# Raw k, q and v of a delta rule turned by transfers and block transposes, in place of TensorE transposes, with the scan two tiles later

## What is computed

```
qkv = silu(causal_depthwise_conv(concat([q, k, v]), conv_w))      # 4 taps along the tokens
q, k = l2_normalize(q) * DN_DK**-0.5, l2_normalize(k)
# in chunks of 64 tokens, g = cumsum(log decay), decay = exp(g_c - g_s) on c >= s
a_mat = strict_lower((k*beta) @ k.T * decay)
u, w = triangular_solve(a_mat + I, [v*beta, k*beta*exp(g)])
qk = (q @ k.T) * decay
# step over the chunks
v_new = u - w @ S ;  o = (q*exp(g)) @ S + qk @ v_new ;  S = S*g_tot + k_tail.T @ v_new
o = rms_norm(o) * silu(z)
```

## Time and profile before

| | us |
|---|---|
| median of 3 runs | 1929.85 (1929.77 to 1930.6) |
| the profiled execution | 1930.64 |
| its span, first to last instruction | 1928.8 |
| TensorE busy | 1913.5 (99%) |
| VectorE busy | 1330.6 (69%) |
| ScalarE busy | 928.9 (48%) |
| GpSimd busy | 101.3 (5%) |

### The profile page before, as it was taken

The page is one execution under the profiler, slowest core; times in us unless marked ns, Lnnn a source line. Parts: engine busy times, 40 slices in busy tenths (PEclk is TensorE's granted clock), DMA queues, the critical chain, the costliest instruction groups (busy, mean ns, idle before and its releaser), DMA issues.

```text
span 1928.8 us, 31440 instructions
## 1 busy us (share of the span) xinstructions
PE 1913.5 (99%) x10359; PEld 1574.6 (82%) x10359; DVE 1330.6 (69%) x1872; ACT 928.9 (48%) x1308; POOL 101.3 (5%) x296
## 2 busy tenths in 40 slices
PE   9999999999999999999999999999999999999997
PEld 7788888888888888888888887888888888888886
DVE  7868688786757777776566756577675466665656
ACT  5555564554455555545544436544443444443442
POOL 0102020010002121212000000000000000000000
PEclk9999999999999999999999999999999999999999
DMA  7555555564655555555666676565666556666655
GB/s 280 165 166 184 182 172 178 167 187 146 201 171 169 179 168 179 166 182 165 206 194 191 214 248 199 175 195 189 193 196 193 191 194 191 196 192 195 196 187 175
DMA packets 103672, 362.57 MB, mean 188 GB/s; under 512 B 11472, under 2 KB 15376, under 8 KB 103440
## 3 DMA queue, kind: packets, MB, share of 16 engines
q1 hardware_dynamic: 97904, 351.65, 56.7%
q10 hardware_dynamic: 5664, 9.46, 1.5%
HBM read 355.28 MB, written 5.78 MB: 187 GB/s over the span
## 4 chain that ended last, share of the span: by engine, by line
PE 92%; DVE 4%; ACT 2%; issue 1%; DMA 0%; SPq 0%; DVEq 0%; ACTq 0%
PE pg L415 86%; PE B L415 4%; DVE wlo L1266 1%; DVE cT L1274 1%; DVE gates L1274 1%; DVE Pm L1266 1%; DVE AT L1266 1%; ACT QKT L959 0%; PE B L513 0%; DMA raw<-in_weights 0%; ACT whi L809 0%; PE B L666 0%; DVE Tc L1457 0%; PE B L538 0%; PE B L631 0%
## 5 line engine op out<-in xcount | busy, mean ns | idle before, releaser
L1266 DVE TENSOR_TENSOR wlo<-raw,whi 128x1024 fp32r<-128x1024 f32 (+1 forms) x640 | 779.2, 1221 | 470.0 <-ACT whi L809 452.2
L809 ACT ACTIVATE whi<-raw 128x1024 fp32r<-128x1024 f32 (+1 forms) x640 | 674.3, 1057 | 700.9 <-PE pg L415 687.1
L415 PE MATMUL pg<-whi,act_x 128*128 128x512 f32 x2960 | 950.0, 395 | 0.7 <-ACT whi L809 0.7
L415 PEld LDWEIGHTS pg<-whi,act_x 128*128 128x128 f32 x2960 | 555.5, 188 | 123.8 <-issue 7.9
L415 PE MATMUL pg<-wlo,act_x 128*128 128x512 f32 x1480 | 574.8, 390 | 0.0
L415 PE MATMUL pg<-whi,act_a 128*128 128x512 f32 x1632 | 504.9, 389 | 0.5 <-DVE act_a L1266 0.3
L415 PEld LDWEIGHTS pg<-whi,act_a 128*128 128x128 f32 x1632 | 306.3, 188 | 64.9 <-DVE act_a L1266 1.3
L415 PEld LDWEIGHTS pg<-wlo,act_x 128*128 128x128 f32 x1480 | 278.3, 188 | 53.7
L415 PE MATMUL pg<-wlo,act_a 128*128 128x512 f32 x816 | 317.5, 389 | 0.0
L415 PEld LDWEIGHTS pg<-wlo,act_a 128*128 128x128 f32 x816 | 153.2, 188 | 31.6
L415 PE MATMUL pg<-whi,act_b 128*128 128x512 f32 x512 | 158.3, 389 | 0.0
(11 more groups left out here) (231 smaller groups left out, 1048.6 us busy)
## 6 DMA issues: line engine op xcount, KB each, us to landing
raw<-in_weights SPq DMA_DIRECT2D x646, 512.0 KB, 4.2
decm<-sums_out ACTq DMA_DIRECT2D x4, 512.0 KB, 4.4
turn_v<-stage ACTq DMA_DIRECT2D x4, 512.0 KB, 2.9
kT<-turn_v ACTq DMA_DIRECT2D x16, 128.0 KB, 2.9
gates<-in_ln_in SPq DMA_DIRECT2D x4, 512.0 KB, 6.0
gates<-in_ln_in SPq DMA_DIRECT2D x1, 2048.0 KB, 8.4
out<-gates SPq DMA_DIRECT2D x8, 256.0 KB, 2.7
turn_o<-stage ACTq DMA_DIRECT2D x3, 512.0 KB, 4.3
```

The costliest lines, as they stand in the source:

```text
L415: return nc.tensor.matmul(o, l, r, start=start, stop=stop)
L809: return nc.scalar.activation(o, i, ACT.Copy, scale=scale)
L1266: return V.tensor_tensor(o, a, b, op)
```

## The change

- TensorE's `turn_conv` and `dn_conv` go. ScalarE copies k, v, q out of PSUM with the columns ordered by blocks of 32 channels, waits for its own copy, and stores all of `hraw` to a DRAM buffer `turn_c`. GpSimd waits for the store and issues four reads (one for each block of 32 channels) into `moved`, which is `qT`'s memory; VectorE turns the 32x32 blocks of `moved` into `rawT` (`vda`'s memory) with one instruction of 128x1024. First tap and products of the convolution read `rawT` in SBUF, not PSUM.
- The block transpose stands in slots 11, 23 and 27, the halves of the convolution in 12, 13 / 24, 25 / 28, 29, each silu one slot after the second half.
- k into token order moves from slot 13 to 15, k k from 14 to 16, the rounds to 19 to 23, the off-diagonal groups to 24 and 25, ScalarE's copies of the inverse to 26, v's blocks to 27, the k q products to 31; `QKT` and the scaling of v move to the next body's slots 0 and 1, the masking of `decm` to slot 9 of the next body (30 in the first), the decay one slot later.
- The scan stands two slots later. Its output is scaled and turned into blocks together in slot 14.
- GpSimd's queue is, for each j: reads of k, the root of the scan's output, the root of k, reads of v, reads of q.

```diff
-CONV_SLOTS = [(8, 10), (16, 18), (24, 26)]
+CONV_SLOTS = [(12, 13), (24, 25), (28, 29)]
+RAW_SLOTS = (11, 23, 27)
-OT_SLOTS = (12, 14)
-O_BLOCKS, V_BLOCKS = 11, 22
+OT_SLOTS = (13, 15)
+O_SCALED, O_BLOCKS, V_BLOCKS = 14, 14, 27
-V_SCALED = (28, 30)
+SCAN = 2
-DECAY = range(4, 8)
+DECAY = range(5, 9)
-GROW = {17: 0, 19: 1, 20: 2, 21: 3, 22: 4}
+GROW = {19: 0, 20: 1, 21: 2, 22: 3, 23: 4}
-OFF_P, OFF_T = 23, 24
+OFF_P, OFF_T = 24, 25
...
+        moved = flat(qT[:, :, :]).rearrange("p (a q i) -> p a q i", a=4, i=SB)
+        rawT = flat(vda[:, :, :]).rearrange("p (h s) -> p h s", h=HB)
...
-            def turn_conv(j, kind, half):
...
-                if s == 13:
+                if s == 15:
                     pe.wait_ge(N["act_silu"], 1 + 3 * j + 1)
...
-                if s == 14:
+                if s == 16:
                     pe.wait_ge(N["act_sqk"], 1 + 2 * j + 2)
                     pe.wait_ge(N["dve_ktail"], 1 + j + 1)
...
-                if s == 28:
+                if s == 31:
                     pe.wait_ge(N["act_silu"], 1 + 3 * j + 3)
...
             def dn_evac(n, i, j):
                 act.wait_ge(tile_used, n)
                 if i < 3:
-                    act.wait_ge(N["pe_conv"], 1 + 6 * j + 2 * i)
-                    rows_out(i % 2, lambda t: hraw[:, t, :])
+                    if i or not isinstance(j, int):
+                        act.wait_ge(c_kept, 16 * (3 * j + i))
+                        act.wait_ge(c_full, 64 * (3 * j + i))
+                    by_channel = flat(hraw[:, :, :]).rearrange("p (b h t i) -> p t h b i", b=4, h=HB, t=TOK)
+                    for t in range(TOK):
+                        last = copy(by_channel[:, t], pg[i % 2][t][:, :].rearrange("p (h b i) -> p h b i", h=HB, b=4))
+                    last.then_inc(evac[i % 2], 1)
+                    act.wait_ge(evac[i % 2], 2 * j + (1, 1, 2)[i])
+                    act.dma_start(turn_c.rearrange("a x b c -> (a x) (b c)"), flat(hraw[:, :, :])).then_inc(c_kept, 16)
...
-                            last = nc.scalar.activation(cT[:, kind, h, :], conv_bank(kind, half)[:, i * SEQ:(i + 1) * SEQ], ACT.Copy,
+                            last = nc.scalar.activation(cT[:, kind, h, :], rawT[:, h, :], ACT.Copy,
...
-                if s == 25:
+                if s == 26:
                     act.wait_ge(N["dve_t"], 1 + 2 * j + 1)
...
+            def conv_moves(j, i):
+
+                pool.wait_ge(c_kept, 16 * (3 * j + i + 1))
+                pool.wait_ge(N["dve_raw"], 1 + 3 * j + i)
+                for b in range(4):
+                    pool.dma_start(moved[b * SB:(b + 1) * SB], turn_c[:, :, b].rearrange("a x (q i) -> x a q i", i=SB)
+                                   ).then_inc(c_full, 16)
+
             for j in range(NB + 1):
+                if j < NB:
+                    conv_moves(j, 0)
...
+                    conv_moves(j, 1)
+                    conv_moves(j, 2)
...
+                if s in RAW_SLOTS:
+                    i = RAW_SLOTS.index(s)
+                    dve.wait_ge(c_full, 64 * (3 * j + i + 1))
+                    dve.wait_ge(N["act_tap"], 1 + 6 * j + 2 * i)
+                    V.transpose(rawT.rearrange("p h (t a x) -> p a (h t) x", t=TOK, x=SB), moved).then_inc(N["dve_raw"], 1)
...
-                            ins = stt(dst, conv_bank(kind, half)[:, i * SEQ:(i + 1) * SEQ - back], w, dst, ALU.mult, ALU.add)
+                            ins = stt(dst, rawT[:, h, 0:SEQ - back], w, dst, ALU.mult, ALU.add)
```

More of the change, by code:

```diff
@@ L190, in build @@
         TT, WT = Pm[:, :, 0:SB], Pm[:, :, SB:CH]
-        def conv_bank(kind, half):
-            return B[1 if kind == 0 and half else 0]
         def bc(ap, n):
@@ L595, in dn_scan @@
             def dn_scan(j, s, alone=False):
+                s -= SCAN
                 if s == 0:
@@ L915, in dn_conv @@
                         half = slots.index(s)
-                        act.wait_ge(N["pe_conv"], 1 + 6 * j + 2 * kind + half + 1)
+                        act.wait_ge(N["dve_raw"], 1 + 3 * j + kind + 1)
                         if half == 0:
@@ L944, in dn_build @@
             def dn_build(j, s):
-                if s == 0 and not isinstance(j, int):
+                if s == 2 and not isinstance(j, int):
                     sums_in(j)
@@ L1012, in dn_scan @@
             def dn_scan(j, s, alone=False):
+                if not alone and s == O_HI:
+                    act.wait_ge(o_full, 64 * (j + 1))
+                    copy(by_block(hi(act_a, HB * j, HB)), by_source(oT)).then_inc(N["act_oT"], 2)
+                s -= SCAN
                 if s == 1:
@@ L1029, in dn_scan @@
                     copy(hi(act_a, HB * j, HB, t * P, (t + 1) * P), B4[2 + t]).then_inc(N["act_oT"], 1)
-                if not alone and s == O_HI:
-                    act.wait_ge(o_full, 64 * (j + 1))
-                    copy(by_block(hi(act_a, HB * j, HB)), by_source(oT)).then_inc(N["act_oT"], 2)
             def body(n, evac_fn, mixes=()):
@@ L1493, in dn_scan @@
             def dn_scan(j, s, ch, alone=False):
+                if s == 0:
+                    for t in range(TOK):
+                        dve.wait_ge(N["pe_kq"], 1 + 2 * j + t + 1)
+                        tt(QKT[:, 4 * t:4 * t + 4, :], B4[3 * t], decm[:, 4 * t:4 * t + 4, :], ALU.mult
+                           ).then_inc(N["dve_qk"], 1)
+                if s == 1:
+                    dve.wait_ge(N["pool_rinv"], 1 + j + 1)
+                    dve.wait_ge(v_full, 64 * (j + 1))
+                    for t in range(TOK):
+                        v_scaled(j, t)
+                if s == O_SCALED:
+                    dve.wait_ge(N["pool_rs"], 1 + j + 1)
+                    for t in range(TOK):
+                        tt(od[:, t], od[:, t], bc(d_("rs")[:, HB * t:HB * (t + 1)], P), ALU.mult
+                           ).then_inc(N["dve_oh"], 1)
+                if not alone and s == O_BLOCKS:
+                    dve.wait_ge(N["dve_oh"], 1 + 2 * j + 2)
+                    dve.wait_ge(v_kept, 16 * (j + 1))
+                    for t in range(TOK):
+                        last = V.transpose(stage[:, :, :, :].rearrange("p b (h t) x -> p h t b x", t=TOK)[:, :, t],
+                                           od[:, t].rearrange("p h (b x) -> p h b x", x=SB))
+                    last.then_inc(N["dve_oS"], 1)
+                if not alone and s == O_HI + 1:
+                    dve.wait_ge(N["act_oT"], 1 + 2 * j + 2)
+                    tt(by_block(lo(act_a, HB * j, HB)), by_source(oT), by_block(hi(act_a, HB * j, HB)), ALU.subtract
+                       ).then_inc(N["dve_oT"], 2)
+                s -= SCAN
                 if s in (0, 3):
@@ L1519, in dn_scan @@
                     seed(d_("rs"), d_("qs")).then_inc(N["dve_qs"], 1)
-                if s == 10:
-                    dve.wait_ge(N["pool_rs"], 1 + j + 1)
-                    for t in range(TOK):
-                        tt(od[:, t], od[:, t], bc(d_("rs")[:, HB * t:HB * (t + 1)], P), ALU.mult
-                           ).then_inc(N["dve_oh"], 1)
-                if not alone and s == O_BLOCKS:
-                    dve.wait_ge(N["dve_oh"], 1 + 2 * j + 2)
-                    dve.wait_ge(v_kept, 16 * (j + 1))
-                    for t in range(TOK):
-                        last = V.transpose(stage[:, :, :, :].rearrange("p b (h t) x -> p h t b x", t=TOK)[:, :, t],
-                                           od[:, t].rearrange("p h (b x) -> p h b x", x=SB))
-                    last.then_inc(N["dve_oS"], 1)
-                if not alone and s == O_HI + 1:
-                    dve.wait_ge(N["act_oT"], 1 + 2 * j + 2)
-                    tt(by_block(lo(act_a, HB * j, HB)), by_source(oT), by_block(hi(act_a, HB * j, HB)), ALU.subtract
-                       ).then_inc(N["dve_oT"], 2)
                 if alone and s - 1 in OT_SLOTS:
```

32 lines of the change are left out of this document (11 added, 21 removed).

## The result

The changed kernel takes 1962.06 us (median of 6 runs, 1958.57 to 1970.46) against 1930.34 (6 runs, 1929.77 to 1931.42): ratio 1.017, 95% interval 1.0147 to 1.0193, slower by 31.7 us. Forecast were 1937 us and a range up to 1949: the sign was right, the size a fifth of what came, and the range missed. The six executions differ by 12 us, and the longer ones have in the main the lower mean granted clock: 1958.57 at 0.996, 1961.96 at 0.990, 1970.46 at 0.987. The profiled execution after took 1967.68 us (0.988), its span 1965.9, 37.1 more than before; so it pays 5.4 us more than the median does, and what follows accounts for the 37.1.

The account below looks back on a forecast made before the run. TensorE, busy in 99% of the span, was taken as the bound. -10.65 - 1.4 + 10.8 + 2.4 + 6.0 = +7.15 us on the profiled 1930.64 gave 1937.8, forecast as 1937 us, range 1925 to 1949.

Parts of the forecast that it names:

- The transposes and the old wait: TensorE's queue: 96 transposes at 0.111 us go, 10.65 us, and 1.4 us of waiting at an inverse round: gain 12.05.
- First place: Last step of the inverse, slot 27: TensorE waits for copies behind v's silu, 2.7 us a body, 10.8 in four.
- Second place: The k q products, slot 31: TensorE waits 0.6 us a body for q's silu, 2.4 in four.
- Third place: k into token order and its squares, slots 15 and 16: k transposes and k k products late, together 6.0 us.
- the mask copies: First body, slots 15 and 16 count: small VectorE copies put at 2 us, in place of the scan's work.
- The reads by GpSimd: Raw k before slot 11: lands after 8.8 to 14.9 us, middle 11.85, needed at 12.6; just in time, cost nothing.
- The convolution from SBUF: VectorE's convolution products: left at 2.60 us a half; nearest row for both inputs in SBUF 479 ns against 476.
- The sum: All terms together, whole kernel: +7.15 us on the profiled 1930.64 us, forecast 1937 us.
- the reads were not late: Rival, slot 11: GpSimd issues slowly, raw k lands late, up to 9.2 us on top, 1946; chance 0.17.
- Only the silu costs: Rival: VectorE catches up before slot 11 and after 26; only 8.2 us at the inverse stays, 1926; chance 0.18.
- all waits are covered: Rival: convolution from SBUF runs so much quicker that the six copies are in time, 1918 us; chance 0.15.

Follow-up runs that it names:

- experiment 5: Kernel before, with each of TensorE's 96 transposes of raw k, v, q issued twice in a row: 1940.13 us, ratio 1.0048.
- Experiment 1: Changed kernel, with ScalarE's six copies of the inverse ahead of v's silu in slot 26: 1947.20 us, ratio 1.0085.
- experiment 2: Changed kernel, with TensorE's loop over bodies 1 to 3 written out: 1952.85 us, ratio 1.0118.
- experiment 12: Changed kernel, with ten unread 512-column matmuls added on TensorE ahead of the waits of slot 27: 1957.94 us, ratio 1.0134.
- 6: Changed kernel, with the masking of decm in the looped bodies moved from slot 9 to 18: 1966.84 us, ratio 1.0184.
- experiment 4: Changed kernel, with GpSimd in the first body waiting for the store of the sums before k's reads: 1963.14 us, ratio 1.0168.
- experiment 8: Changed kernel: inverse copies before v's silu, loop written out, masking, sums wait, decay and scan-output blocks later, raw q's transpose earlier: 1936.19 us, ratio 1.0024.
- experiment 9: Changed kernel, with the twelve block reads of a body issued by ScalarE in place of GpSimd: 1965.74 us, ratio 1.0172.
- 3: Kernel before, with only the k q products moved from slot 28 to 31 and QKT to the next body's slot 0: 1936.65 us, ratio 1.0031.
- 10: Kernel before, with only v turned by store, reads and block transpose, and steps in slots 17 to 31 rearranged: 1928.87 us, ratio 0.9989.
- 11: Kernel before with v alone turned by transfers, plus the split of the scan's turned output moved to slots 27 and 28: 1929.83 us, ratio 0.9992.

## Why the prediction was wrong, by its steps

*The transposes and the old wait, -12.05:* right. 0.107 us each against 0.111 (experiment 5); no round of the inverse waits in the changed kernel, but for 0.23 us in the first body.

*First place, 2.7 us a body:* right, 2.57 (10.3 us for 10.8), by the chain that was given: convolution, silu, six copies. Experiment 1 shows it.

*Second place, 0.6 a body:* right in size (0.52 in experiments 2 and 12), but in the changed kernel it measured nothing: the slow tile behind each 64x64 group gives VectorE the time. Where that tile ran at the full clock, the wait was there (two bodies of experiment 2, one of 6, four of 12).

*Third place, 6.0 us:* sized too low; it measured 12.5. In the looped bodies 1.6 and 0.55 stand for the 0.5 and 0.8 predicted. The count reached the end of k's silu 22.3 us after tile 8's start, with the transposes due at 21.8; the silu ended at 23.0 (from 277.2 to 300.2), and TensorE was there at 21.5. In the first body 0.3 and 1.8 were predicted, and 4.60, 1.29 and 0.23 measured: there ScalarE waits from 42.3 to 48.3 for the store of the sums, with the roundings of tiles behind it. The prediction counted the mask copies, not this store, which took 1.8 us before and 7.5 with k's transfer beside it. How much of the first body's waits is the store's stays open: experiment 4 had it land in 4.1 us and won 0.7 of the 5.9; experiment 8, which waits for it two slots later, brought the 4.60 down to 2.10 and the 1.29 to nothing.

*The reads by GpSimd, in time and free:* right (experiment 9). An issue took 0.56 us, inside the bounds of 0.40 and 1.20, and the reads landed 3.3 us later. The convolution from SBUF takes 479 ns a product, as the nearest row had it.

*The sum:* here it failed, by two terms that it does not have. The k q group was moved from 28 to 31 and priced only by what it needs, not by what stands behind it, the loop's jump: 7.8 us of idle time (experiments 2 and 3). And each wait was priced at its own length, as if the tile behind it cost what a tile costs at the full clock. By start times it took 1.5 to 2.9 us more after each of seven of them; by the granted clock they cost 17.5 us together (experiment 12 shows the cause). With the waits as they came and these two terms left out, the time would have been 1937 + (22.8 - 19.2) = about 1941. The other 21 us lie in what was not counted, and no rival had it either. (The profiled execution shows 7.8 + 17.5 = 25.3 of it, since it ran 5.6 us above the median at a lower clock.)

*The rivals:* the reads were not late, since no idle time stands ahead of raw k's transpose (experiment 9). "Only the silu costs" and "all waits are covered" are both out: VectorE didn't catch up before slot 11, it worked without a pause from 279.8 to 300, but for 0.19 us.

It stays open why the gap at the jump is 1.5 in one place and 3.7 in another, and why the clock falls at one idle time of 2.58 us and not at the next. A version with k in its old place and q as well as v turned was not tried; I expected q's reads to land too late for a k q group far from the jump.

## What to carry to other kernels

Price a wait of TensorE at more than its length: behind most idle times of TensorE of about 2 us or more the next tile ran at half clock here, and in the profiled execution 22.7 us of such waits cost 17.5 us more. Since it isn't the same in each execution, take several before a difference of a few us is believed. When a step is moved, look at what it comes to stand beside in the instruction stream, the loop's jump above all, and not only at what it waits for. Offload kind by kind: v, with idle slots on the receiving engine, paid back a little (-1.9 us, in part by the new places of its steps). k, in crowded slots, saved 3.4 us of transposes, and its steps and what was moved beside them waited 12.5; k alone was not run.

## What the runs showed of the hardware that wasn't expected

- A jump of TensorE's loop cost nothing when three tiles stood between it and the last small group (the kernel before), 1.3 to 1.6 us with two (experiments 10 and 11), and 1.5 to 4.5 with none (experiments 3 and 9, the changed kernel).
- The granted clock fell to 0.50 at each idle time of 2.57 us or more in the changed kernel, at 17 of 20 of 2.57 or 2.58 over five kernels, and at some of 1.83 to 2.04 in experiment 8; the spacing of 512-column matmuls went from 0.23 to 0.43 us.
- A 16 KB store landed in 1.8 us in the kernel before, in 4.1 with k's store of 512 KB issued 5.5 us ahead of it (experiment 4), and in 7.5 with four block reads of 128 KB beside it as well (the changed kernel). GpSimd needed 0.56 us to issue one of these reads, ScalarE about 0.46 (four in 1.84 us).
